# A split-precision feed-forward on one core: high and low rows streamed as 256 columns each, or as 512 together

## The reference

```
def swiglu(x, w_gate, w_up, w_down):
    return (jax.nn.silu(x @ w_gate) * (x @ w_up)) @ w_down
```

## Time and profile before

| | |
|---|---|
| median of 3 runs | 1085.41 us (1084.77 to 1091.42) |
| the profiled execution, its own time | 1087.59 us |
| its span, first to last instruction | 1085.9 us |
| mean granted TensorE clock | 0.987 of full speed |
| TensorE busy, share of the span | 98% |
| VectorE, ScalarE, GpSimd busy | 64%, 48%, 9% |
| second feed-forward, third feed-forward (pairs after the first) | about 368 to 537 us, about 904 to 1070 us |

### The profile page before, as it was taken

How to read it: one execution, slowest core, us unless ns; L and a number is a source line. 1 busy time by engine, 2 the same in 40 slices (tenths; PEclk the granted TensorE clock), 3 DMA queues, 4 the chain that set the end, 5 groups by cost and what they waited for, 6 DMA issues and landing times.

```text
span 1085.9 us, 20307 instructions
## 1 busy us (share of the span) xinstructions
PE 1063.9 (98%) x8823; PEld 1032.5 (95%) x8823; DVE 698.5 (64%) x699; ACT 516.2 (48%) x559; POOL 92.6 (9%) x90
## 2 busy tenths in 40 slices
PE   8999999999999999999999999999999989999997
PEld 7999999999999999999998888999979989999997
DVE  7665565756858665565699665776636657655552
ACT  6544444636565544444575554313332665444344
POOL 3000000100202100000036500000000021000001
PEclk9999999999999999999999999989998989999999
DMA  9666556465536466656546433323323453665541
GB/s 318 201 212 200 193 185 201 152 198 162 178 127 203 147 206 220 193 188 198 164 135 193 137 100 110 124 78 117 117 79 117 155 194 121 229 196 190 193 155 39
DMA packets 147192, 179.89 MB, mean 166 GB/s; under 512 B 3965, under 2 KB 134258, under 8 KB 147138
## 3 DMA queue, kind: packets, MB, share of 16 engines
q1 hardware_dynamic: 146464, 177.55, 50.5%
q0 software_dynamic: 400, 1.43, 0.4%
q10 hardware_dynamic: 274, 0.13, 0.0%
HBM read 178.05 MB, written 1.05 MB: 165 GB/s over the span
## 4 chain that ended last, share of the span: by engine, by line
PE 86%; DVE 7%; ACT 5%; issue 2%; DMA 0%; DVEq 0%; ACTq 0%; SPq 0%
PE ps L1398 26%; PE ps L1399 25%; PE ps L1400 25%; ACT w_hi L1052 2%; PE ps L1758 2%; DVE w_lo L1215 2%; PE ps L1716 1%; PE ps L1715 1%; ACT ar L341 1%; DVE w_lo L1207 1%; DMA stage<-in_ffn_w_gate_dram 0%; ACT L1028 0%; PE ps L1797 0%; PE ps L1738 0%; PE ps L1795 0%
## 5 line engine op out<-in xcount | busy, mean ns | idle before, releaser
L1215 DVE TENSOR_TENSOR w_lo<-stage,w_hi 128x2048 fp32r<-128x2048 f32 x164 | 378.7, 2313 | 196.3 <-ACT w_hi L1052 196.3
L1398 PE MATMUL ps<-x_hi,w_lo 128*128 128x256 f32 (+1 forms) x1480 | 419.5, 283 | 6.8 <-DVE x_lo L1221 2.0
L1399 PE MATMUL ps<-x_lo,w_hi 128*128 128x256 f32 (+1 forms) x1480 | 415.1, 280 | 0.0
L1400 PE MATMUL ps<-x_hi,w_hi 128*128 128x256 f32 (+1 forms) x1480 | 414.9, 280 | 0.0
L1052 ACT ACTIVATE w_hi<-stage 128x2048 fp32r<-128x2048 f32 x164 | 311.5, 1905 | 208.6 <-PE ps L1400 206.9
L1398 PE MATMUL ps<-a_hi,w_lo 128*128 128x256 f32 (+1 forms) x1112 | 310.7, 279 | 3.2 <-DVE a_lo L1221 2.2
L1399 PE MATMUL ps<-a_lo,w_hi 128*128 128x256 f32 (+1 forms) x1112 | 309.4, 278 | 0.0
L1400 PE MATMUL ps<-a_hi,w_hi 128*128 128x256 f32 (+1 forms) x1112 | 309.3, 278 | 0.0
L1398 PEld LDWEIGHTS ps<-x_hi,w_lo 128*128 128x128 f32 x1480 | 281.3, 190 | 14.0 <-issue 9.2
L1400 PEld LDWEIGHTS ps<-x_hi,w_hi 128*128 128x128 f32 x1480 | 281.3, 190 | 0.0
L1399 PEld LDWEIGHTS ps<-x_lo,w_hi 128*128 128x128 f32 x1480 | 281.0, 190 | 0.1
(11 more groups left out here) (297 smaller groups left out, 849.9 us busy)
## 6 DMA issues: line engine op xcount, KB each, us to landing
stage<-in_w_in_dram SPq DMA_DIRECT2D x36, 1024.0 KB, 5.3
stage<-in_ffn_w_up_dram SPq DMA_DIRECT2D x22, 1024.0 KB, 5.3
stage<-in_ffn_w_down_dram SPq DMA_DIRECT2D x22, 1024.0 KB, 5.0
stage<-in_w_ffn_in_dram SPq DMA_DIRECT2D x22, 1024.0 KB, 5.1
stage<-in_ffn_w_gate_dram SPq DMA_DIRECT2D x21, 1024.0 KB, 5.4
stage<-in_w_ffn_out_dram SPq DMA_DIRECT2D x11, 1024.0 KB, 4.9
stage<-in_w_gate_dram SPq DMA_DIRECT2D x8, 1024.0 KB, 5.4
stage<-in_w_out_dram SPq DMA_DIRECT2D x8, 1024.0 KB, 5.1
```

The lines of the kernel that those rows point to most:

```text
L1215: nc.vector.tensor_tensor(o, i, b.bitcast(F32), ALU.subtract).then_inc(s["lo_ready"], 1)
L1398: nc.tensor.matmul(o, wl, xh, start=start, stop=False, skip_group_check=skip)
L1399: nc.tensor.matmul(o, wh, xl, start=False, stop=False, skip_group_check=skip)
L1400: return nc.tensor.matmul(o, wh, xh, start=False, stop=stop, skip_group_check=skip)
```

## The change

1. The high and low parts of the input, `a_hi` and `a_lo`, were two tensors. They become the two halves of `a_both`, chunk by chunk, so that `a_wide` sees 512 columns in a row: 256 high, 256 low.
2. For `f` = 1 and 2 the gate and up slabs after the first pair use the new `wide_slab`. In each block one matmul streams the 512 columns against the high weights, and one streams the 256 high columns against the low weights into the first half. The bank's first half is then high by high plus low by high, the second half is weight high by input low. A block is two matmuls with 512 and 256 columns, where it was three with 256.
3. A slab now fills two whole banks, one for each column chunk: gate always banks 0 and 1, up always 2 and 3. TensorE waits for the scaling of the pair just before.
4. ScalarE copies the second halves of the two banks to `ga_s` or `up_s`. VectorE adds the first halves, and then multiplies by the norm's factor out of SBUF.
5. TensorE's loop of five iterations becomes one pair, four iterations and one pair. Down slabs, the first pair, the first feed-forward and the mixers compute as before; some of the mixers' views of `a_hi` and `a_lo` are written as two runs of 256.

```
-        a_hi = sb("a_hi", [P, DC, SEQ], F32R)
-        a_lo = sb("a_lo", [P, DC, SEQ], F32R)
+        a_both = sb("a_both", [P, DC, 2, SEQ], F32R)
+        a_hi, a_lo = a_both[:, :, 0, :], a_both[:, :, 1, :]
+        a_wide = a_both[:].rearrange("p c two t -> p c (two t)")
...
# ScalarE, gate and hidden
+                    elif f > 0:
+                        act.wait_ge(s["slab_used"], up(m + 1, it))
+                        nc.scalar.activation(pair(ga_s), ps[:, 0:2, SEQ:], ACT.Copy).then_inc(s["gate_copied"], 1)
...
+                    if f > 0 and J > J0:
+                        act.wait_ge(s["slab_used"], up(m + 1, it))
+                        nc.scalar.activation(pair(up_s), ps[:, 2:4, SEQ:], ACT.Copy).then_inc(s["up_copied"], 1)
...
# VectorE, gate (hidden has the same with up_s and banks 2:4)
+                    if f > 0 and not first:
+                        dve.wait_ge(s["gate_copied"], up(J - PAIRS - f + 1, it, 2))
+                        nc.vector.tensor_tensor(pair(ga_s), pair(ga_s), ps[:, 0:2, 0:SEQ], ALU.add).then_inc(s["gate_summed"], 1)
+                        dve.wait_ge(s["gate_summed"], up(J - PAIRS - f + 1, it, 2))
+                        nc.vector.tensor_tensor(pair(ga_s), pair(ga_s), bc2, ALU.mult).then_inc(s["gate_scaled"], 1)
+                        split_lo(m + 3, it)
+                        return
...
# TensorE
+            def wide_slab(n, bank, it=None):
+
+                slab_ready(n, it)
+                wh, wl = wview(w_hi, n, DC), wview(w_lo, n, DC)
+                for c in range(2):
+                    for k in range(DC):
+                        nc.tensor.matmul(ps[:, bank + c, :], wh[:, k, P * c:P * c + P], a_wide[:, k, :], start=k == 0, stop=k == DC - 1,
+                                         skip_group_check=True)
+                        last = nc.tensor.matmul(ps[:, bank + c, 0:SEQ], wl[:, k, P * c:P * c + P], a_hi[:, k, :], start=False, stop=k == DC - 1,
+                                                skip_group_check=True)
+                last.then_inc(s["slab_used"], 1)
...
+                    def three_slabs(J, m, it=None, first=False):
+                        if not first:
+                            pe.wait_ge(s["gate_scaled"], up(J, it, 2))
+                        wide_slab(m, 0, it)
+                        if first:
+                            pe.wait_ge(s["std_ready"], rec)
+                        else:
+                            pe.wait_ge(s["up_scaled"], up(J, it, 2))
+                        wide_slab(m + 1, 2, it)
+                        if first:
+                            pe.wait_ge(s["y_zeroed"], f + 1)
+                        down_slab(f, m + 2, J - 1, it=it)
+
+                    three_slabs(J0 + 1, n + 2, first=True)
+                    with pe.Fori(0, (PAIRS - 3) // 2) as it:
+                        for b in range(2):
+                            three_slabs(J0 + 2 + b, n + 5 + 3 * b, it)
+                    three_slabs(J0 + PAIRS - 1, n + 3 * PAIRS - 4)
```

More of the change, by code:

```diff
@@ L186, in ffn_input @@
         def ffn_input(f):
-            return (x_hi[:, :, X0:], x_lo[:, :, X0:]) if f == 0 else (a_hi[:], a_lo[:])
+            return (x_hi[:, :, X0:], x_lo[:, :, X0:]) if f == 0 else (a_hi, a_lo)
         def hidden_part(f, part, J):
@@ L231, in program, with kv_part @@
         r_q, r_kv = sq_flat[:, 1056:1056 + SEQ], sq_flat[:, 1312:1312 + L2]
-        def kv_part(v):
-            return v[:].rearrange("p c t -> p (c t)")[:, 512:512 + 2 * L2].rearrange("p (c t) -> p c t", c=2)
+        def kv_part(part):
+            at = 4 * SEQ + 2 * L2 * part
+            return a_both[:].rearrange("p c two t -> p (c two t)")[:, at:at + 2 * L2].rearrange("p (c t) -> p c t", c=2)
         R2 = rstd[:, 1, :]
@@ L297, in attn_hi @@
                 act.wait_ge(s["pv1_mm"], g + 1)
-                nc.scalar.activation(a_hi[:, 2 * g:2 * g + 2, :].rearrange("p c t -> p (c t)"), ps[:, 4, :],
+                nc.scalar.activation(a_hi[:, 2 * g:2 * g + 2, :], pair(ps[:, 4, :]),
                                      ACT.Copy).then_inc(s["attn_hi"], 1)
@@ L496, in pair_hi @@
                 act.wait_ge(s["pv2_mm"], p + 1)
-                nc.scalar.activation(a_hi[:, 2 * p:2 * p + 2, :].rearrange("p c t -> p (c t)"), ps[:, 7, :],
+                nc.scalar.activation(a_hi[:, 2 * p:2 * p + 2, :], pair(ps[:, 7, :]),
                                      ACT.Copy).then_inc(s["mla_hi"], 1)
@@ L629, in pair_lo @@
                 dve.wait_ge(s["mla_hi"], p + 1)
[L630 to L631 removed]
+                nc.vector.tensor_tensor(a_lo[:, 2 * p:2 * p + 2, :], pair(ps[:, 7, :]),
+                                        a_hi[:, 2 * p:2 * p + 2, :].bitcast(F32),
                                         ALU.subtract).then_inc(s["mla_lo"], 1)
@@ L1245, in hidden @@
                     dve.wait_ge(s["slab_used"], up(m + 1, it))
-                    nc.vector.tensor_tensor(pair(up_s), ps[:, 6:8, 0:SEQ] if first else pair(ps[:, 2 + J % 2, :]), bc2,
-                                            ALU.mult).then_inc(s["up_scaled"], 1)
+                    if f > 0 and not first:
+                        dve.wait_ge(s["up_copied"], up(J - PAIRS - f + 1, it, 2))
+                        nc.vector.tensor_tensor(pair(up_s), pair(up_s), ps[:, 2:4, 0:SEQ], ALU.add).then_inc(s["up_summed"], 1)
+                        dve.wait_ge(s["up_summed"], up(J - PAIRS - f + 1, it, 2))
+                        nc.vector.tensor_tensor(pair(up_s), pair(up_s), bc2, ALU.mult).then_inc(s["up_scaled"], 1)
+                    else:
+                        nc.vector.tensor_tensor(pair(up_s), ps[:, 6:8, 0:SEQ] if first else pair(ps[:, 2 + J % 2, :]), bc2,
+                                                ALU.mult).then_inc(s["up_scaled"], 1)
                     dve.wait_ge(s["up_scaled"], up(J + 1, it, 2))
```

29 lines of the change are left out of this document (16 added, 13 removed).

## The result

The changed kernel has a median of 1100.02 us (1097.29 to 1101.9, 4 runs), where the kernel before, run beside it, has 1085.09 us (1084.13 to 1091.42, 4 runs). The ratio on record is 1.0117 (the quotient of the two medians is 1.0138), with a 95% interval of 1.0088 to 1.0147: slower by 1.2%. The profiled execution took 1101.9 us, 14.3 us more than that of before, and its span is 1099.8 us, 13.9 us more.

The account below looks back on a forecast made before the run. TensorE's matmul stream and late low weights were taken as the bound. Blocks +2.1 us and feed-forward starts +3.0 us gave +5.1 us on 1085.4 us, so 1090.5 us, with a range of 1081 to 1098 us.

Parts of the forecast that it names:

- rival 2: Second and third feed-forward: slow pace holds to the end in blocks and down slabs; +12.3 us, 1097.7 us, chance 0.15.
- What bounds it: Feed-forwards: only TensorE's matmul cost in the stream (113.3 ns at 256 columns) and late low weights count.
- The price of a block: Wide gate and up slabs: 230.0 + 113.3 = 343.3 ns a block for 340.0, +2.1 us over 640 blocks.
- my upper bound: Wide slabs' blocks: both matmuls at the slow pace, 230.0 + 117.8 = 347.8 ns, +5.0 us.
- My lower bound: Wide slabs' blocks: a fixed excess per start, 219.9 ns at 512 columns, 333.2 ns a block, -4.4 us.
- rival 1: Wide slabs: the 512-column stream is cheaper by the saved start; -1.4 us, 1084.0 us, chance 0.3.
- The pace of everything else: Matmuls outside the wide blocks, such as down slabs: stay at 113.3 ns for 256 columns, so no added cost.
- the condition I set for rival 2: Feed-forward starts: new waits restart TensorE into the slow pace; over 1% slower once it covers 85% of both stretches.
- The start of a feed-forward: First slabs: late low parts make TensorE wait 0.2 to 0.3, then 1.3 us; 1.5 us each, 3.0 us in all.
- The hidden eviction work: Steady pairs: added copy (0.6 us) and add (0.69 us) stay hidden, with at least 2.5 us to spare after gate and up.
- rival 3: Steady pairs: splitting becomes the bound and each pair stalls on a low part; 1100.5 us, chance 0.05.
- my doubts about order: Steady pairs: a wait on `gate_scaled` or `up_scaled` would disprove the order of work; 8.9 and 8.1 us to spare expected.

Follow-up runs that it names:

- experiment 1: Changed kernel with each 512-column matmul cut back into two of 256, eviction work kept; 1091.63 us, ratio 1.0042 to the kernel before.
- experiment 3: Changed kernel without ScalarE's copies and VectorE's adds, 512-column matmuls kept; 1102.91 us, ratio 1.0137 to the kernel before.
- Experiment 5: Changed kernel with eight 512-column matmuls first, then eight of 256, in each column chunk; 1099.62 us, ratio 1.011 to the kernel before.
- experiment 11: The kernel before, unchanged, run and profiled again; 1090.18 us, ratio 1.0002, 117.8 ns in both feed-forwards.
- experiment 2: Kernel of experiment 1 with only the fourth pair's gate slab wide in each of the two feed-forwards; 1100.39 us, ratio 1.0122.
- experiment 7: Kernel of experiment 1 plus one short TensorE wait ahead of the fourth pair's up slab; 1098.37 and 1101.35 us, ratio 1.0104.
- experiment 12: Kernel of experiment 7, unchanged, run and profiled again; 1098.8 us, ratio 1.0125.
- experiment 8: Kernel of experiment 1 plus groups of spare matmuls on a slab's real weights, most after a short wait; one execution, blocks of three 353.3 or 340.0 ns.
- T: Spare block of three 256-column matmuls in experiment 8; its five groups took 353.3, 353.3, 353.3, 340.0 and 340.0 ns a block.
- experiment 9: Kernel of experiment 7 plus one spare 512-column matmul in the slab behind the wait; 1097.1 us, ratio 0.9974 to the kernel before.
- experiment 4: Kernel of experiment 1 plus 12 groups of spare matmuls of many widths, input chunks stationary; one execution, 226.7 ns at 512 columns.

## Why the prediction was wrong about the size

The forecast was 1090.5 us, the range 1081 to 1098, the likeliest outcome "within 1%". The kernel is slower by 1.2%: the median of 1100.0 us lies 2 us above the range, and 1.0117 x 1085.41 is 1098.1. The outcome is rival 2's, which I priced at 1097.7 us and gave 0.15. That its price is so near is in part luck: it has 5.0 us for the blocks, where 8.5 were measured, and its 12.3 us lie 2.0 below the 14.3 of the profiled executions.

**What bounds it: right.** TensorE's stream and the low weights at the start are the only two things that cost. The profiles of both experiments that part them (1 and 3) say so.

**The price of a block: the step that failed.** I took 230.0 + 113.3 = 343.3 ns; it is 353.3 ns in every steady block, 5.5 ns above my upper bound of 347.8. The two numbers came from uniform streams, 512 after 512 and 256 after 256, and I added them as if a matmul's distance were its own. In turn they are 235.3 and 118. Experiment 5 shows how much of the miss is alternation: in groups of eight a block is 346.7 ns, 3.4 over my sum and 6.6 under the measured one. The term is 640 x 13.3 = +8.5 us and not +2.1. My lower bound (219.9 ns at 512) fell too: 512 in a row took 226.7 ns with the input as stationary operand and 233.3 with weights, so rival 1 had no base. Of the width itself the Trainium skill ("TensorE: Matmul & The Clock Gate", section Back-to-back issue gap) gives about 131 ns for each matmul in a sustained stream with 512 columns, with no type named. The trace does not agree for fp32r: no sustained stream here came under 226.7.

**The pace of everything else: the second part of the same failure.** Down slabs at 113.3 ns were taken as given. They run at 118 behind wide slabs: +4.3 us in all by rival 2's own sum, less 0.8 for those already slow. I had seen the two paces and even wrote that a restart sets them, but read "nearly all at the fast one" from a single profiled execution as a property of the kernel. It was one outcome: experiment 11 has the same program at the slow one. And the condition I set for rival 2 was wrong: I wanted the new waits to cause the slow pace. In the changed kernel it is there from the first wide slab, ahead of any of the new waits, and in experiment 2 sixteen wide matmuls bring it in the middle of a fast stretch without a wait.

**The start of a feed-forward: right.** 1.5 us each was predicted; the profiles of experiments 1 and 3 give 1.5 to 1.9. The two waits in TensorE's timeline of the changed kernel:

```profile
385.67 0.50 PE L1455 MATMUL ps<-a_both,w_hi 128*128 128x512 f32 x1 [0.21 <-DVE w_lo L1223]
...
392.60 0.50 PE L1455 MATMUL ps<-a_both,w_hi 128*128 128x512 f32 x1 [1.02 <-DVE w_lo L1223]
```

0.21 and 1.02 us, for 0.2 to 0.3 and 1.3, at the places named.

**The hidden eviction work: right.** ScalarE's copy takes 595 ns (0.6 taken). There are no waits on a low part in the steady pairs and none on `gate_scaled` or `up_scaled`, so rival 3 and my doubts about order are out. A pair, from one gate add on VectorE to the next in the changed kernel's timeline:

```profile
444.40 0.69 DVE L1248 TENSOR_TENSOR ar<-ar,ps 128x512 f32<-128x512 f32 x1 [1.70 <-ACT ar L1083]
...
461.36 0.69 DVE L1248 TENSOR_TENSOR ar<-ar,ps 128x512 f32<-128x512 f32 x1 [1.62 <-ACT ar L1083]
```

is 16.96 us, where I said 16.4 and the earlier trace rows has 16.32. The add starts when the copy ends, and that wait lies beside TensorE's stream.

**The sum, with the sizes measured.** For each feed-forward: 320 x 13.3 ns = 4.3 us, 2.2 less 0.4 for the down slabs, 1.5 for the start: 7.6 us, where the trace has 7.4 and 7.1. Twice that on the profiled execution is 15.2 for a measured 14.3.

**What stays open.** What the two paces are was not settled. At both, the weight load starts 3 to 4 ns after the matmul ahead of it, and what differs is the time from there to the next matmul, 110 against 114 ns. The same wait in the same program brought both (experiments 7 and 12). Nor is the moment of the restart a sign that I can read: in experiment 8 the first distance behind it was 221 and 222 ns in two slow groups of T and 223 and 224 in the two fast ones, but in the same trace two later groups that begin with T have 226 ns there and run slow, and the real slab behind the last group has 221 ns and runs fast. Nor is it settled why alternation of two lengths has only the slow one. The first profile of the changed kernel also has 1.4 us more in front of the second mixer's slabs, with the clock at half for 3.4 us there; the second profile does not have it, so the change does not bring it each time. Code that no edit touches also differs from profile to profile: the part up to the second feed-forward's norm took 366.2 to 372.4 us in the kernels without spare groups, the second mixer's part 349.5 to 354.6. Medians that differ by a few us are therefore not explained one by one.

## What to carry to other kernels

Price a matmul by the sequence it stands in: two lengths in turn can cost more than the sum of what each costs among its own kind (353.3 against 346.7 ns here), and can leave the pace of unchanged code behind them changed. One profile shows one outcome; where it has two paces for identical instructions at the same clock, take a second profile of the kernel before ahead of any claim of 1%, since here that alone is worth 9 us. Look first for what the wider matmul is to save: with weights as the stationary operand 512 columns in a row cost 233.3 ns and twice 256 at the fast pace 226.7, so there was nothing to buy with the added eviction.

## What the runs showed that I had not expected

- The same program, at full granted clock, runs 256-column matmuls at 113.3 or at 117.8 ns for a whole feed-forward, 5.5 us apart, and its pace can change at a restart of TensorE or behind one 512-column matmul, in both directions (experiments 7, 8, 9 and 12).
- 512 and 256 columns in turn took 353.3 ns a pair in every stretch that I looked at: two profiles of the changed kernel and experiments 2, 3, 4 and 8.
- 192 and 224 columns both took 111.6 ns, so below some 236 columns (an estimate: there N/2.4 + 13.3 gives 111.6) another cost than the columns sets the distance. The Trainium skill ("TensorE: Matmul & The Clock Gate", section LDWEIGHTS (loading the stationary operand)) puts the load of 128 columns of weights at P/1.2, 106.7 ns. The floor is near that and 5 ns above it; that the load is what sets it was not tested.
- The operands matter: with chunks of the input as the stationary one, 256 columns took 120.0 ns and 512 in a row 226.7 (experiment 4); with the weights they took 113.3 or 117.8, and 233.3 (experiment 8). Why was not tested.
